# Expert tokens by GpSimd's indirect transfers through DRAM, in place of selection matmuls

## The reference

```
def _moe(h, router, w_gate_up, w_down):          # h: (1, 256, 1024), already normed
    top_v, top_i = lax.top_k(h @ router, 2)       # 8 experts, two per token
    gates = softmax(top_v)                        # spread over 8 columns: gate_full
    for e in range(8):
        g, u = split(h @ w_gate_up[e])            # 1024 x 7168
        y = y + gate_full[..., e] * ((silu(g) * u) @ w_down[e])   # 3584 x 1024
    return y                                      # x = x + y, then a final RMSNorm
```

## Time and profile before

| | us |
|---|---|
| median of 3 runs | 1656.31 |
| lowest and highest | 1655.06 and 1656.72 |
| the profiled execution | 1656.18 |
| its span, from the first to the last instruction | 1654.4 |

### The profile page before, as it was taken

How to read it: one execution, slowest core, us unless ns; L and a number is a source line. 1 busy time by engine, 2 the same in 40 slices (tenths; PEclk the granted TensorE clock), 3 DMA queues, 4 the chain that set the end, 5 groups by cost and what they waited for, 6 DMA issues and landing times.

```text
span 1654.4 us, 22146 instructions
## 1 busy us (share of the span) xinstructions
PE 1622.1 (98%) x8139; PEld 1339.8 (81%) x8139; DVE 1205.2 (73%) x969; ACT 1015.3 (61%) x837; POOL 86.6 (5%) x107
## 2 busy tenths in 40 slices
PE   8999999999899999999999999999999999999996
PEld 6888888899699877888888888888888888888885
DVE  4554454454654568888888887887888887887886
ACT  5444443433633466767767777777777777777774
POOL 0000000050331220000000000000000000000000
PEclk9999999999999999999999999999999999999998
DMA  9555555476166417999999999999999999998992
GB/s 364 164 181 181 194 182 178 153 248 195 68 202 205 153 52 244 357 367 319 363 360 320 360 361 324 356 361 322 357 362 321 358 362 321 362 358 325 358 361 87
DMA packets 234392, 457.74 MB, mean 277 GB/s; under 512 B 9008, under 2 KB 15152, under 8 KB 234336
## 3 DMA queue, kind: packets, MB, share of 16 engines
q1 hardware_dynamic: 231216, 454.06, 78.9%
q10 hardware_dynamic: 3120, 2.91, 0.6%
HBM read 455.86 MB, written 1.08 MB: 276 GB/s over the span
## 4 chain that ended last, share of the span: by engine, by line
PE 95%; DVE 2%; ACT 1%; issue 1%; DMA 0%; SPq 0%; ACTq 0%; DVEq 0%
PE bY L273 9%; PE bY L275 9%; PE bY L274 9%; PE bG L273 8%; PE bG L274 8%; PE bG L275 8%; PE bU L275 8%; PE bU L274 8%; PE bU L273 8%; PE bS L274 3%; PE bS L275 3%; PE bS L273 3%; PE bT L493 2%; DVE logit L1155 1%; PE bX L275 1%
## 5 line engine op out<-in xcount | busy, mean ns | idle before, releaser
L263 DVE TENSOR_TENSOR wlo<-raw,whi 128x2048 fp32r<-128x2048 f32 x427 | 979.9, 2295 | 364.7 <-ACT whi L257 362.3
L257 ACT ACTIVATE whi<-raw 128x2048 fp32r<-128x2048 f32 x427 | 818.6, 1917 | 471.1 <-PE bY L275 182.2
L273 PE MATMUL bU<-whi,eTh 128*128 128x512 f32 x448 | 181.4, 405 | 0.0
L273 PE MATMUL bG<-whi,eTh 128*128 128x512 f32 x448 | 178.9, 399 | 1.1 <-ACT eTl L772 1.1
L273 PE MATMUL bY<-whi,hTh 128*128 128x512 f32 x448 | 179.0, 400 | 0.0
L274 PE MATMUL bG<-whi,eTl 128*128 128x512 f32 x448 | 178.7, 399 | 0.0
L275 PE MATMUL bG<-wlo,eTh 128*128 128x512 f32 x448 | 178.5, 398 | 0.0
L274 PE MATMUL bU<-whi,eTl 128*128 128x512 f32 x448 | 177.6, 396 | 0.0
L274 PE MATMUL bY<-whi,hTl 128*128 128x512 f32 x448 | 177.5, 396 | 0.0
L275 PE MATMUL bU<-wlo,eTh 128*128 128x512 f32 x448 | 177.5, 396 | 0.0
L275 PE MATMUL bY<-wlo,hTh 128*128 128x512 f32 x448 | 177.4, 396 | 0.0
(11 more groups left out here) (384 smaller groups left out, 2390.4 us busy)
## 6 DMA issues: line engine op xcount, KB each, us to landing
raw<-in_m_w_gate_up_dram SPq DMA_DIRECT2D x224, 1024.0 KB, 5.1
raw<-in_m_w_down_dram SPq DMA_DIRECT2D x112, 1024.0 KB, 5.0
raw<-in_b_w_in_dram SPq DMA_DIRECT2D x36, 1024.0 KB, 5.0
raw<-in_f_w_gate_up_dram SPq DMA_DIRECT2D x28, 1024.0 KB, 5.1
raw<-in_f_w_down_dram SPq DMA_DIRECT2D x14, 1024.0 KB, 4.9
raw<-in_a_w_in_dram SPq DMA_DIRECT2D x4, 1024.0 KB, 11.1
raw<-in_a_w_out_dram SPq DMA_DIRECT2D x4, 1024.0 KB, 14.0
biasrev<-toeplitz SPq DMA_DIRECT2D x32, 128.0 KB, 4.6
```

What stands on the lines that cost most here:

```text
L257: nc.scalar.activation(whi[:, t % CUT], raw[:, t % RAW], ACT.Copy).then_inc(hi_done, 1)
L263: nc.vector.tensor_tensor(wlo[:, t % CUT], raw[:, t % RAW], whi[:, t % CUT].bitcast(F32), ALU.subtract).then_inc(lo_done, 1)
L273: pe.matmul(dst, a[0], b[0], start=start, stop=False)
```

## The change

For the first seven items (`direct`) the tokens no longer go through `sel` matmuls. Once, ahead of the items, GpSimd scales `hn` to the normed tokens and writes them to a DRAM tensor `normed` (two transfers of 512 KB), and writes `x` to a DRAM tensor `summed` (two such transfers, and a third that fills 128 spare rows). For each item two small products with `sel` (`slot_rows`, four columns) give each slot's token number, whether the slot is used, and its gate; VectorE turns them into row numbers `to_rows` and `from_rows` and a factor `slot`. GpSimd gathers the next item's 128 rows from `normed` into `e_tok` by an indirect transfer; TensorE transposes them (`turn_tokens`), ScalarE and VectorE cut them. The item's result is scaled by its gate in `y_cut` on ScalarE and goes to `y_out`; GpSimd adds it to the rows of `summed` by an indirect transfer that accumulates. Unused slots go to the spare rows. Before the eighth item's result is added, `summed` is loaded back into `x`. The eighth item, and any after it, keeps spread and `add_item`; the first item's gather stays too. The number of further items is loaded into a register after the seventh item rather than before the first. There are now three bodies in the program of TensorE, ScalarE and VectorE: the seven direct items' loop, the loop of further items, and the last.

```diff
-            for t in (selT, yh, yl):
-                last = nc.gpsimd.memset(t[:].bitcast(F32), 0.0)
-            last.then_inc(y_lo, 1)
-
+            pool.wait_ge(hnh_done, 2)
+            pool.wait_ge(hnl_done, 2)
+            for tb in range(NT):
+                nc.gpsimd.tensor_scalar(hn[:, tb], hn[:, tb], rstd[:, tb:tb + 1], None, ALU.mult).then_inc(hn_done, 1)
+            for tb in range(NT):
+                pool.wait_ge(hn_done, 3 + tb)
+                pool.dma_start(hn_dram[tb * P:tb * P + P, :], hn[:, tb]).then_inc(hn_out, 16)
+            for r in range(NT + 1):
+                pool.dma_start(acc_dram[r * P:r * P + P, :], x[:, r % NT]).then_inc(acc_done, 16)
+
+            pool.wait_ge(hn_out, 32)
+            for i in range(E - 1):
+                pool.wait_ge(from_ready, i + 1)
+                nc.gpsimd.indirect_dma_start(e_tok[:], None, hn_dram,
+                                             bass.IndirectOffsetOnAxis(from_rows[:, 0:1], 0)).then_inc(e_full, 16)
+                pool.wait_ge(slot_ready, i + 1)
+                pool.wait_ge(y_hi, 2 * i + 2)
+                pool.wait_ge(acc_done, 48 + 16 * i)
+                nc.gpsimd.indirect_dma_start(acc_dram, bass.IndirectOffsetOnAxis(to_rows[:, 0:1], 0), y_out[:],
+                                             None, compute_op=ALU.add).then_inc(acc_done, 16)
+            pool.wait_ge(acc_done, 48 + 16 * (E - 1))
+            for tb in range(NT):
+                pool.dma_start(x[:, tb], acc_dram[tb * P:tb * P + P, :]).then_inc(x_back, 16)
...
+            def slot_rows(n, c):
+
+                for tb in range(NT):
+                    mm = pe.matmul(X[:, c:c + 4], sel[:, tb, :], tab[:, tb, bass.ds(n, 1), :], start=tb == 0,
+                                   stop=tb == NT - 1)
+                mm.then_inc(ix_psum, 1)
+
+            def turn_tokens(i):
+
+                pe.wait_ge(e_full, i * 16 + 16)
+                for b, bank in enumerate((G, U)):
+                    for kk in range(4):
+                        kb = 4 * b + kk
+                        mm = pe.transpose(bank[:, kk * P:kk * P + P], e_tok[:, kb * P:kb * P + P], ident[:])
+                    mm.then_inc(ga_psum, 1)
...
-                    if j == 0:
-                        spread(1, i * 2)
...
+                    if j == 1 and direct:
+                        pe.wait_ge(tab_ready, 1)
+                        slot_rows(i, 0)
+                    if j == 3 and direct:
+                        pe.wait_ge(pick_ready, i + 2)
+                        slot_rows(i + 1, 8)
...
+                        if n == 1 and qn == 3 and direct:
+                            turn_tokens(i)
+                        if n == 1 and qn == 1 and not direct:
+                            pe.wait_ge(selT_ready, m + 1)
+                            spread(0, m * 2)
...
-            with pe.Fori(0, ITEMS - 1) as i:
-                with pe.If(i < n_last):
-                    item_body(i)
+            with pe.Fori(0, E - 1) as i:
+                item_body(i)
+            pe.wait_ge(ids_ready, 1)
+            m_last = pe.value_load(ids[0:1, 0:1], min_val=0, max_val=OVER)
...
+                    if direct:
+                        act.wait_ge(slot_ready, i + 1)
+                        act.wait_ge(acc_done, i * 16 + 48)
+                        copy(y_out[:, sl], (Y0, Y1)[n][:], y_hi, scale=slot[:, 0:1])
...
+                    if t == DOWN + DT + 4 and direct:
+                        for b, bank in enumerate((G, U)):
+                            act.wait_ge(ga_psum, i * 2 + 5 + b)
+                            copy(eTh[:, 4 * b:4 * b + 4].rearrange("p k t -> p (k t)"), bank[:], ga_hi)
...
-                    if j == 0:
-                        add_item(1, i * 2, i)
...
+                        if direct:
+                            dve.wait_ge(ix_psum, i * 2 + 1)
+                            dve.wait_ge(acc_done, i * 16 + 48)
+                            slot_rows(i)
...
+                    if j == 4 and direct:
+                        dve.wait_ge(ix_psum, i * 2 + 2)
+                        nc.vector.tensor_copy(from_rows[:, 0:1], X[:, 8:9]).then_inc(from_ready, 1)
```

More of the change, by code:

```diff
@@ L71, in encoder @@
             b_w_in, b_w_out, f_w_gate_up, f_w_down, m_router, m_w_gate_up, m_w_down,
-            c_ident, c_pool, c_bucket, c_band, c_class, c_tri, c_iota, out):
+            c_ident, c_pool, c_bucket, c_band, c_class, c_tri, c_iota, c_tab, c_dump, out):
     with ExitStack() as ctx:
@@ L168, in encoder @@
         msilu, mh = mbuf[:, 0], mbuf[:, 1]
+        at_y = top[0]
         yh = place("yh", [D], F32R)
@@ L175, in encoder @@
         idx = place("idx", [NT, 8], U32)
+        tab = place("tab", [NT, E, 4], F32R)
+        dump = place("dump", [2], F32)
+        slot = place("slot", [1], F32)
+        got = place("got", [6], F32)
+        to_rows = place("to_rows", [1], I32)
+        from_rows = place("from_rows", [1], I32)
+        tab_in = place("tab_in", [NT, E, 2], F32)
+        end_moe, top[0] = top[0], at_y
+        y_out = place("y_out", [D], F32)
+        e_tok = place("e_tok", [D], F32)
+        top[0] = end_moe
         G, U, T, X, Y0, Y1, S0, S1 = (psum(n) for n in ("bG", "bU", "bT", "bX", "bY0", "bY1", "bS0", "bS1"))
         toep_dram = nc.dram_tensor("toeplitz", (HEADS, 512), F32, kind="Internal").ap()
+        hn_dram = nc.dram_tensor("normed", (S, D), F32, kind="Internal").ap()
+        acc_dram = nc.dram_tensor("summed", (S + P, D), F32, kind="Internal").ap()
         x_in_done = sem("x_in_done")
         spare_zero = sem("spare_zero")
-        c_in = [sem(f"const{i}") for i in range(13)]
+        c_in = [sem(f"const{i}") for i in range(15)]
         raw_full = [sem(f"raw_full{i}") for i in range(RAW)]
@@ L915, in _ @@
                     load_const((C_GAIN3, C_GAIN4))
+                    act.wait_ge(pv_done, 2 * (HH // 2))
+                    load_const((C_TAB, C_DUMP))
                 ahead(t0 + 18)
@@ L966, in item_body @@
                     ahead(4 * j + 2)
-                    if j == 1:
-                        act.wait_ge(selT_psum, i + 1)
+                    if j == 1 and not direct:
+                        act.wait_ge(selT_psum, m + 1)
                         copy(selT[:].rearrange("p t s -> p (t s)"), X[:, 0:S], selT_ready)
@@ L1336, in item_body @@
                 for t in range(DOWN, FFN_TILES):
-                    if t == FFN_TILES - 1:
+                    if t == FFN_TILES - 1 and not direct:
                         y_cut(1)
@@ L1341, in item_body @@
                         hidden_lo(SLABS - 1)
-                    if t == DOWN + DT - 1:
+                    if t == DOWN + DT - 1 and not direct:
                         y_cut(0)
                     if t == DOWN + DT + 4:
-                        add_item(0, i * 2 + 1, i + 1)
-            with dve.Fori(0, ITEMS - 1) as i:
-                with dve.If(i < n_last):
-                    item_body(i)
+                        if direct:
+                            for b, bank in enumerate((G, U)):
+                                dve.wait_ge(ga_hi, i * 2 + 3 + b)
+                                f = lambda t: t[:, 4 * b:4 * b + 4].rearrange("p k t -> p (k t)")
+                                lo(f(eTl), bank[:], f(eTh), ga_lo)
+                        else:
+                            add_item(0, m * 2, i + 1)
+                if not direct and not last:
+                    add_item(1, m * 2 + 1, i + 1)
+            with dve.Fori(0, E - 1) as i:
+                item_body(i)
+            m_last = dve.value_load(ids[0:1, 0:1], min_val=0, max_val=OVER)
+            with dve.Fori(0, OVER) as m:
+                with dve.If(m < m_last):
+                    item_body(m + (E - 1), m)
                 with dve.Else():
                     dve.nop()
-            item_body(n_last, last=True)
-            dve.wait_ge(sc_psum, n_last * 2 + 3)
-            dve.wait_ge(x_added, n_last * 2 + 3)
+            item_body(m_last + (E - 1), m_last, last=True)
+            dve.wait_ge(sc_psum, m_last * 2 + 2)
+            dve.wait_ge(x_added, m_last * 2 + 2)
             for tb in (1, 0):
                 sl = x[:, tb, 512:D]
-                nc.vector.scalar_tensor_tensor(sl, (S0, S1)[tb][:], gate_item[:, tb, bass.ds(n_last + 1, 1)], sl,
+                nc.vector.scalar_tensor_tensor(sl, (S0, S1)[tb][:], gate_item[:, tb, bass.ds(m_last + E, 1)], sl,
                                                ALU.mult, ALU.add).then_inc(x_final, 1)
```

125 lines of the change are left out of this document (80 added, 45 removed).

## The result

| | before | after |
|---|---|---|
| median of 7 runs, us | 1656.02 | 1648.43 |
| lowest and highest | 1654.39 and 1656.72 | 1639.10 and 1652.05 |
| the profiled execution | 1656.18 | 1648.55 |
| its span | 1654.4 | 1646.7 |

The ratio is 0.9945, with a 95% interval of 0.993 to 0.996: faster by 7.6 us where 27 were forecast. The runs of the changed kernel lie on two levels, two near 1639 us and five at 1648 to 1652; the profile is of the upper one.

The account below looks back on a forecast made before the run. TensorE, busy for 98% of the span, was taken to bound the kernel. The terms -39.2 + 5.5 + 3.0 + 1.2 + 1.0 + 1.0 = -27.5 us turn 1656.2 into 1629; own range 1625 to 1644, overall 1623 to 1660.

Parts of the forecast that it names:

- The mechanism that was to gain: In the items, spreads, gather halves and `sel` turns leave TensorE: 39.2 us together; an item's period falls by 4.2.
- the moved register load: Between the seventh and eighth item: costs 1.2 us, from nothing if queued matmuls cover it to 3.6.
- At the first item nothing is won: Register load's old place: removing it gains nothing, since TensorE waits there for the first tokens' copies anyway.
- The start of the block: GpSimd's two scalings of `hn` beside VectorE's first cuts: 1.0 us taken, from 0 to 4.8.
- VectorE at j = 2: Four small operations ahead of `pick` in each item: 1.0 us taken, from 0 to 6.6.
- GpSimd holding VectorE up by its indirect transfers: Rival: making each indirect transfer keeps VectorE off, TensorE loses 1.3 us 14 times, 19 us: 1647; chance 0.18.
- the inference that the prediction takes from the Trainium skill: Making descriptors needs the write interface, which VectorE's two-input instruction doesn't take; so GpSimd's transfers would not hold VectorE up.
- Loads behind: Rival: accumulations halve the weight loads' rate for 25 us, loads come 3 us too late, seven times 21: 1650; chance 0.06.
- The late accumulation: Rival: VectorE at j = 2 waits for an accumulation beyond 34 us, six times; at 45 us 1695; chance 0.16.
- the nearer of the two bounds: Landing time of an accumulation: 5.3 us as for a plain 512 KB transfer, against a far bound of 33.6.
- The last line of the prediction: Sign of a wrong forecast: TensorE's idle time in the block passes 10 us.

Follow-up runs that it names:

- e5b: The changed kernel with TensorE's code behind the seven items written twice, as in e5a, and the scalings of `hn` on ScalarE, as in e4; 1627.28 us.
- e2: The changed kernel without the loop of further items on TensorE, ScalarE and VectorE, the register load staying at its new place; 1629.94 us.
- e1: The changed kernel with the register load of TensorE, ScalarE and VectorE put back ahead of the loop of the seven items; 1649.63 us.
- e5a: The changed kernel with TensorE's code behind the seven items written twice, so that without further items nothing is jumped over; 1630.04 us.
- e4: The changed kernel with the two scalings of `hn` on ScalarE in place of GpSimd; 1646.43 us.
- e8: The changed kernel with two rounds of the loop of further items in place of three, on TensorE, ScalarE and VectorE; 1649.14 us.
- e10: The changed kernel with 128 empty instructions at the start of TensorE's program, which are not in the compiled program; 1648.92 us.
- e9: The changed kernel with the three rounds of the loop of further items kept, but TensorE's body in them empty; 1630.69 us.

## Why the prediction was wrong

*The mechanism that was to gain: right.* The period fell by 4.0 us where 4.2 were forecast. The transposes of `e_tok` take 745.71 - 744.91 = 0.80 for eight, and the block's inner items have no TensorE wait over 0.3 us. TensorE's timeline, and the row of the slot products by line:

```profile
744.91 0.60 PE L741 MATMUL bG<-ident,e_tok 128*128 128x128 f32 x4
745.35 0.60 PE L741 MATMUL bU<-ident,e_tok 128*128 128x128 f32 x4
745.71 0.47 PE L291 MATMUL bY<-whi,hTh 128*128 128x512 f32 x1
...
L731 PE MATMUL bX<-tab,sel x28: 251/251/251, 648.9 to 1409.0; 128*128 x28
```

With the two losses taken away e5b has 1627.28 us, and e2, with only the first away, 1629.94: the forecast of 1629 and its own range are met, but by kernels other than the one it was made for.

*The step that failed: "the moved register load".* The prediction took 1.2 us at the new place, 3.6 at most. It priced the load and looked no further at what else the moved lines are. The load costs nothing there (e1). Right behind it stands the second loop, three times a jump over a body that never ran: 17.1 us and 2.1 more at the lower clock, which is nearly all of the 1648.43 - 1629 = 19.4 us by which the forecast was missed. The sum had no term for branches that skip. The kernel before has three skipped rounds as well, but over the body that has just run seven times, and no gap there, so the trace of before could not show the price; the bound should have been left wide for that reason. "At the first item nothing is won" holds for the time, but not for the reason given: TensorE does start sooner without the load (e1), and VectorE's late cut takes it back.

*The start of the block: undersized.* It took 1.0 us with bounds of 0 to 4.8. Moving the scaling away was worth 2.8 us (e5a to e5b), inside the bounds. Wrong was the duration: GpSimd's scalings took 4.7 us each, not the 2.4 of the two-input operation in the earlier trace rows, and it was not the weight tiles but the small operations in front of them that were held up. The Trainium skill (SBUF — State Buffer, section "Who interferes with whom") has both engines share ports that one of them holds to the end of its instruction, for VectorE's two-input operations and for some modes of `tensor_scalar`. That GpSimd holds VectorE up agrees with e4. That it does so for two-input operations up to its end does not show: two cuts of VectorE within GpSimd's 9.39 us took 4.49 us, as long as before.

*VectorE at j = 2: 1.0 us taken, nothing measured.* The four operations take some 0.65 us (911.37 to 912.01) and are covered: TensorE waits for nothing there.

*The rivals.* GpSimd holding VectorE up by its indirect transfers is empty: no cut over 2.70 us, though making one takes 1.8 to 2.8 us of GpSimd; the inference that the prediction takes from the Trainium skill agrees. Loads behind: none, with 1.5 us more to landing. The late accumulation: 9.3 us of the 34 that it had; the nearer of the two bounds was the one to go by. For that landing the prediction's estimate by the Trainium skill (DMA: Bandwidth & Descriptors, section "Anatomy of one DMA — SWDGE (gpsimd) path"), 3.2 us, is too short, since the runs show 8.7 and 9.3.

*The last line of the prediction* named what would prove it wrong: TensorE idle for over 10 us in the block. It was 16.95 + 4.87 us, in the two places above.

## What to carry to other kernels

When a loop is split or a special case gets a body of its own, price the code that is skipped as well as the code that runs: put the common path so that it falls through, with rare bodies behind it, above all on the engine that sets the time and has the longest body. A gap that the profile puts down to "issue", with all operands ready, is looked for in the instruction stream, and the page's count of instruction packets, then their count in the gap's own window, is the first thing to compare. Before a small operation is given to GpSimd, look at what VectorE does at that moment, not only at whether GpSimd is free.

## What the runs showed that was not expected

- A loop that does nothing cost 18.5 us of 1648 (e2), and the same code between 5.4 and 18.1 us in TensorE's gap by where it lay and when it came, in steps of some 6 us with a packet of instructions at the start of each.
- A second round over a skipped body cost some 13.6 us (17.33 against 3.76), a third nothing (16.95).
- The changed kernel has runs near 1639 us among those near 1649 (two of 7; in e8 three of 10, in e10 one of 5), while e2, e9, e5a and e5b, without the gap, spread by under 1.7 us each. No profile is of such a run, so what is shorter in it is open.
- Further waits cost TensorE time though they are met already: its first matmuls start at 15.17 us with 58 of them and at 22.29 with 128, which is 0.10 us for each instruction.
- Indirect transfers of 128 rows of 4 KB landed after 8.7 us (gather) and 9.3 (accumulation) beside weight loads, with 368 GB/s moved in all.
